# Hybrid mixer: 24 modulation slabs multiplied and halved on GpSimd instead of summed on VectorE

## The reference, cut to what matters

```python
c_act = jax.nn.silu(c)
mod = (c_act @ ada_w[l] + ada_b[l])[:, None, :]
sh_m, sc_m, gt_m, sh_f, sc_f, gt_f = jnp.split(mod, 6, axis=-1)
h = rms_norm(x, norm_mix[l]) * (1 + sc_m) + sh_m
y = hybrid_mixer(h, ...)
x = x + gt_m * y
h = rms_norm(x, norm_ffn[l]) * (1 + sc_f) + sh_f
```

## Time and profile before

| What | Value |
|---|---|
| Median of 3 runs | 3048.45 us (3048.13 to 3048.93) |
| The profiled execution, its own time | 3045.3 us |
| Its span, first to last instruction | 3043.5 us |
| Mean granted TensorE clock | 0.979 |
| Start of the program | 0 to about 50 us |
| Hybrid mixer | about 50 to 508 us |

### The profile page before, as it was taken

The page is one execution under the profiler, slowest core; times in us unless marked ns, Lnnn a source line. Parts: engine busy times, 40 slices in busy tenths (PEclk is TensorE's granted clock), DMA queues, the critical chain, the costliest instruction groups (busy, mean ns, idle before and its releaser), DMA issues.

```text
span 3043.5 us, 32382 instructions
## 1 busy us (share of the span) xinstructions
PE 2888.6 (95%) x13454; PEld 2310.1 (76%) x13454; DVE 1419.6 (47%) x2227; ACT 955.4 (31%) x1276; POOL 442.6 (15%) x345
## 2 busy tenths in 40 slices
PE   6989969999998999999999999899999999999998
PEld 4767657788887878877888877678888865688886
DVE  4474575567534333333232444645444454544353
ACT  3344323321223231233222333432223334332222
POOL 1011011210112211221101100012112100012022
PEclk9999979999999999999999999999999999999999
DMA  5210212446422222222532322112232321122321
GB/s 217 83 56 29 76 56 90 178 161 230 171 81 103 87 73 92 78 83 85 164 110 87 114 77 68 53 69 93 94 111 71 110 68 45 61 98 80 120 80 66
DMA packets 49810, 294.30 MB, mean 97 GB/s; under 512 B 6346, under 2 KB 6474, under 8 KB 23809
## 3 DMA queue, kind: packets, MB, share of 16 engines
q1 hardware_dynamic: 43632, 274.48, 25.2%
q0 software_dynamic: 4736, 15.43, 1.9%
q10 hardware_dynamic: 1296, 2.32, 0.2%
HBM read 283.56 MB, written 8.65 MB: 96 GB/s over the span
## 4 chain that ended last, share of the span: by engine, by line
PE 86%; DVE 7%; ACT 4%; DMA 1%; issue 1%; POOL 0%; SPq 0%; DVEq 0%; ACTq 0%
PE ps L218 86%; DVE ada L399 1%; ACT F L1117 1%; DVE wlo L211 1%; DMA Rf<-in_ada0h 1%; PE ps L1141 1%; DVE F L356 0%; DVE hl L360 0%; DMA F<-in_ada 0%; ACT hh L369 0%; ACT whi L200 0%; DVE F L1108 0%; ACT F L1158 0%; DVE F L2048 0%; DVE F L1153 0%
## 5 line engine op out<-in xcount | busy, mean ns | idle before, releaser
L218 PE MATMUL ps<-hh,whi 128*128 128x512 f32 x2088 | 830.4, 398 | 32.1 <-DVE hl L360 14.5
L218 PE MATMUL ps<-hl,whi 128*128 128x512 f32 x2088 | 819.0, 392 | 0.0
L218 PE MATMUL ps<-hh,wlo 128*128 128x512 f32 x2088 | 818.4, 392 | 0.0
L211 DVE TENSOR_TENSOR wlo<-raw,whi 128x2048 fp32r<-128x2048 f32 (+2 forms) x235 | 492.4, 2096 | 572.4 <-ACT whi L200 567.3
L218 PE MATMUL ps<-R,whi 128*128 128x512 f32 x2080 | 650.6, 392 | 7.8 <-DVE wlo L211 2.8
L200 ACT ACTIVATE whi<-raw 128x2048 fp32r<-128x2048 f32 (+2 forms) x235 | 410.0, 1745 | 727.1 <-PE ps L218 727.0
L218 PEld LDWEIGHTS ps<-hh,whi 128*128 128x128 f32 x2088 | 395.6, 189 | 129.8 <-issue 26.0
L218 PEld LDWEIGHTS ps<-R,whi 128*128 128x128 f32 x2080 | 391.2, 188 | 95.1 <-issue 6.7
L218 PEld LDWEIGHTS ps<-hl,whi 128*128 128x128 f32 x2088 | 395.4, 189 | 84.0
L218 PEld LDWEIGHTS ps<-hh,wlo 128*128 128x128 f32 x2088 | 396.0, 190 | 82.1 <-issue 2.2
L218 PE MATMUL ps<-R,wlo 128*128 128x512 f32 x1040 | 405.2, 390 | 0.0
(11 more groups left out here) (315 smaller groups left out, 2512.2 us busy)
## 6 DMA issues: line engine op xcount, KB each, us to landing
F<-in_ada SPq DMA_DIRECT2D x32, 1024.0 KB, 4.8
raw<-in_fs0in SPq DMA_DIRECT2D x22, 1024.0 KB, 5.4
raw<-in_fs1in SPq DMA_DIRECT2D x22, 1024.0 KB, 4.7
raw<-in_fc0in SPq DMA_DIRECT2D x22, 1024.0 KB, 4.7
raw<-in_fc1in SPq DMA_DIRECT2D x22, 1024.0 KB, 4.7
Rf<-in_ada0h SPq DMA_DIRECT2D x24, 512.0 KB, 3.5
raw<-in_fs0out SPq DMA_DIRECT2D x16, 704.0 KB, 4.6
raw<-in_fs1out SPq DMA_DIRECT2D x16, 704.0 KB, 4.0
```

The costliest lines, as they stand in the source:

```text
L211: e.tensor_tensor(m.wlo[n % 2][:, 0:size], m.raw[m.slot[n]][:, 0:size], m.whi[n % 2][:, 0:size].bitcast(F32), SUB).then_inc(*s.up("wlo", n))
L218: return e.matmul(out, l, r, start=start, stop=stop, skip_group_check=True)
```

## The change

The 24 slabs move from DVE to POOL. For one slab POOL makes one multiply of 128x(8x128), with `csil` broadcast along the 128 columns, written in place, then three adds that halve the block: 4x128, 2x128 and 1x128 columns, the last into `ada`. Each waits for the one before. PE's sum and the bias come once per two slabs. The next load is issued when the last add of a slab has ended. In the plan an ada pair is `pool:4.9 dma:3.4`, `pool:4.9`, `pe:0.3 dve:0.2 dma:3.1`; "dma" is an engine with its own clock, and the chain may begin at 13 us of the plan instead of 1. In the start, `norm 2` is put ahead of the first slab's `whi` and `wlo` on ACT and DVE, and "scale 3" and "turn 3" on PE are put between k = 3 and k = 4 of the mixer's first tiles.

```diff
-    for what in ("scale 0", "scale 1", "norm 0", "scale 2", "norm 1", "slab 0", "norm 2", "scale 3", "norm 3"):
+    for what in ("scale 0", "scale 1", "norm 0", "scale 2", "norm 1", "norm 2", "slab 0", "scale 3", "norm 3"):
...
+def pe_start_end(e, s, m, ready):
+
+    def first_ready(k):
+        if k == 4:
+            pe_start_scale(e, s, m, 3)
+            pe_start_turn(e, s, m, 3)
+        ready(k)
+    return first_ready
...
 def ada_steps():
-    for j in range(16, 41):
-        yield step("pe:0.2 dve:0.2", ("six", "mod", "h", j - 1) if j > 16 else None)
-        if j < 40:
-            yield step("dve:1.8")
-            yield step("dve:1.8")
+    for j in range(16, 40, 2):
+        yield step("pool:4.9 dma:3.4")
+        yield step("pool:4.9")
+        yield step("pe:0.3 dve:0.2 dma:3.1", ("six", "mod", "h", j + 1))
...
-    at, ready, free = [0] * 5, [0.0, 1.0, 1.0, 1.0, 1.0], {"pe": 0.0, "act": 0.0, "dve": 0.0, "pool": 0.0}
+    at, ready, free = [0] * 5, [0.0, 1.0, 1.0, 13.0, 1.0], {"pe": 0.0, "act": 0.0, "dve": 0.0, "pool": 0.0, "dma": 0.0}
...
 def pe_ada_chain(e, s, m):
...
+    for j in range(16, 40, 2):
+        yield from steps(2)
+        six_free(s, "mod", "h", j + 1)
+        s.wait_ge("ada_h", "h", j, 7)
+        pe_ada(e, s, m, j // 2 % 2, 2, 6, ("h", j + 1), "ada_h")
+        yield
...
+def pool_ada_chain(e, s, m):
+    w = m.Rf[:, 4 * T:6 * T].rearrange("p (k n) -> p k n", k=8)
+    for j in range(16, 40):
+        a = m.ada[j // 2 % 2][:, P * (j % 2):P * (j % 2) + P]
+        s.wait_ge("ada_in", j)
+        e.tensor_tensor(w, w, m.csil[:, :].unsqueeze(2).to_broadcast([P, 8, P]), MUL).then_inc(*s.up("ada_h", "h", j, 0))
+        for i, n in ((1, 4), (2, 2)):
+            s.wait_ge("ada_h", "h", j, i - 1)
+            e.tensor_tensor(w[:, 0:n, :], w[:, 0:n, :], w[:, n:2 * n, :], ADD).then_inc(*s.up("ada_h", "h", j, i))
+        s.wait_ge("ada_h", "h", j, 2)
+        s.wait_ge("ada_sum", *(("h", (j - 4) // 2 * 2 + 1) if j >= 20 else ("first", 3)))
+        e.tensor_tensor(a, w[:, 0, :], w[:, 1, :], ADD).then_inc(*s.up("ada_h", "h", j, 7))
+        yield
+        if j % 2:
+            yield
```

More of the change, by code:

```diff
@@ L404, in dve_ada, with pe_ada @@
             yield
-def pe_ada(e, s, m, acc, n, bank, key):
-    s.wait_ge("ada_k", *key, 7)
+def pe_ada(e, s, m, acc, n, bank, key, done="ada_k"):
+    s.wait_ge(done, *key, 7)
     for c in range(n):
@@ L464, in act_start @@
     act_start_norm(e, s, m, 1)
+    act_start_norm(e, s, m, 2)
     act_slab(e, s, m, 0)
-    act_start_norm(e, s, m, 2)
     act_row(e, s, m, 3)
@@ L541, in pe_start @@
     for what in ("shift 0", "squares 0", "shift 1", "scale 0", "turn 0", "shift 2", "scale 1", "turn 1", "scale 2", "turn 2",
-                 "shift 3", "scale 3", "turn 3"):
+                 "shift 3"):
         what, i = what.split()
@@ L555, in pe_start, with pe_start_scale, pe_start_turn @@
         elif what == "scale":
-            if i >= 2:
-                s.wait_ge("mod", "first", i - 2)
-            pe_ada(e, s, m, i % 2, 2, 3 + i % 2, ("first", i))
-        else:
[L560 to L565, removed]
+            pe_start_scale(e, s, m, i)
+        else:
+            pe_start_turn(e, s, m, i)
+def pe_start_scale(e, s, m, i):
+    if i >= 2:
+        s.wait_ge("mod", "first", i - 2)
+    pe_ada(e, s, m, i % 2, 2, 3 + i % 2, ("first", i))
+def pe_start_turn(e, s, m, i):
+    if i >= 2:
+        s.wait_ge("mod", "shift", i - 2)
+    s.wait_ge("mod_row", i)
+    for c in range(2):
+        t = mm(e, m.ps[5 + i % 2][:, c:c + 1], first_row(m, i)[:, c * P:(c + 1) * P], m.k("ones")[0:1, 0:1])
+    t.then_inc(*s.up("mod_turn", i))
+def pe_start_end(e, s, m, ready):
[5 more added lines that the diff above has]
+    return first_ready
 FFN = {"s0": ("fs0", 0, False), "s1": ("fs1", 1, False), "c0": ("fc0", 0, True), "c1": ("fc1", 1, True)}
@@ L1993, in pe_gdn_pre @@
         pe_dense_free(s, m, n)
-        yield from pe_tiles(e, s, m, n, (0, 1), m.h, ready)
+        if n == 0:
+            yield from pe_tiles(e, s, m, n, (0, 1), m.h, pe_start_end(e, s, m, ready))
+        else:
+            yield from pe_tiles(e, s, m, n, (0, 1), m.h, ready)
         yield from steps(2)
@@ L2302, in act_gdn_head @@
     if h == 2:
-        s.wait_ge("ada_k", "h", 39, 7)
+        s.wait_ge("ada_h", "h", 39, 7)
     e.activation(m.o(h)[0], qT, ACT.Copy).then_inc(*s.up("o_hi", "hyb", h))
@@ L2671, in dve_ada_chain @@
 def dve_ada_chain(e, s, m):
-    for j in range(16, 41):
-        if j > 16:
-            dve_ada_bias(e, s, m, j - 1, 1, 6, "ada_sum", ("h", j - 1))
+    for j in range(16, 40, 2):
+        yield from steps(2)
+        dve_ada_bias(e, s, m, j, 2, 6, "ada_sum", ("h", j + 1))
         yield
[L2676 to L2680, removed]
+def pool_ada_chain(e, s, m):
[12 more added lines that the diff above has]
+        if j % 2:
@@ L2681, in dve_ada_chain @@
             yield
 def sp_ada_chain(e, s, m):
+    s.wait_ge("mod_mm", 3)
+    s.wait_ge("ada_k", "first", 3, 7)
+    sp_ada(e, s, m, 16)
     for j in range(16, 40):
[L2686 to L2693, removed]
+        yield
+        if j < 39:
+            s.wait_ge("ada_h", "h", j, 7)
+            sp_ada(e, s, m, j + 1)
+        if j % 2:
+            yield
@@ L2699, in pe_hybrid, with sp_ada @@
+def sp_ada(e, s, m, j):
+    e.dma_start(m.Rf[:, 4 * T:6 * T], m.dram["ada0h"][j - 16]).then_inc(*s.dma("ada_in", j))
 def pe_hybrid(e, s, m):
@@ L2703, in act_hybrid @@
 def act_hybrid(e, s, m):
-    merged(act_gdn(e, s, m, 0), act_gdn(e, s, m, 1), act_stick(e, s, m), steps(73), act_gdn_gates(e, s, m))
+    merged(act_gdn(e, s, m, 0), act_gdn(e, s, m, 1), act_stick(e, s, m), steps(36), act_gdn_gates(e, s, m))
 def dve_hybrid(e, s, m):
@@ L2711, in pool_hybrid @@
 def pool_hybrid(e, s, m):
-    merged(pool_gdn(e, s, m, 0), pool_gdn(e, s, m, 1), pool_stick(e, s, m), steps(73), steps(len(GATE_STEPS)))
+    merged(pool_gdn(e, s, m, 0), pool_gdn(e, s, m, 1), pool_stick(e, s, m), pool_ada_chain(e, s, m), steps(len(GATE_STEPS)))
 def sp_hybrid(e, s, m):
```

## The result

The changed kernel takes 3030.33 us in the median of four runs (3026.43 to 3033.55), the kernel before 3048.29 us: a ratio of 0.9941, with a 95% interval of 0.9924 to 0.9958, or 18 us faster. The forecast was 20 us, 3028 us. The profiled execution is the slowest of the four, 3033.55 us for a span of 3031.7 us, so the trace shows 11.8 of the 18 us.

A forecast was written before the change was run, and what follows sets the result against it. The prediction took PE, busy 95% of the span, as the bound, idling most from 376 to 508 us; -4.3 (start) + 3 (early stretch) - 18.9 (last stretch) = -20.2 us gave 3028 us, range 3006 to 3046 us.

The forecast's parts named there:

- The sum: Whole program: start -4.3, early stretch +3 and last stretch -18.9 give -20.2 us, so 3028 us against the median.
- The start: Before the mixer's first tiles: PE does k = 0 to 3 in its 8.59 us gap, gaining 4.3 us.
- the cover: In the start: k = 6 and 7 wait for `norm 3`, which is late next if the gap no longer hides it.
- POOL's cost: A slab's multiply and three adds on POOL: 5.1 us, or a period of about 8.9 us with its load.
- The early stretch: Mixer, 100 to 350 us: POOL work stalls DVE while slabs leave it; between -5 and +4 us, taken as +3.
- the lock's rival: Early stretch: every POOL microsecond stops DVE, +15 instead of +3, so -8 in all, 3040 us; chance 0.17.
- The last stretch: Mixer, 376 to 508 us: L2067 10.9 us, slabs inside DVE bursts 5 us, clock 3 us; together -18.9 us.
- No slab after 350 us: Sign of being right: no POOL slab after about 350 us, all fourteen slabs out of the last stretch.
- PE standing for POOL's sums: Rival: load and POOL outlast the 9.05 us a slab PE's queue expects; at 11 us, 3075 us; chance 0.12.
- The reserve of 9.05 us a slab: Plan's 8.3 us a slab with queues 9% behind, against the forecast 8.9; PE's wait for sums costed at nothing.
- The plan's order: All queues: new costs reorder them, which no row can price; 10 us allowed to either side.

The follow-up runs named there:

- start_only: The kernel before with the changed start alone (norm 2 ahead of the first slab's split, scale 3 and turn 3 between k = 3 and k = 4): 3044.21 us, ratio 0.9999.
- after_again: The changed kernel itself measured once more, on another chip: 3030.76 us, ratio 0.9944.
- pool_short: The changed kernel without each slab's multiply and first two adds, so the modulation's second half is not computed: 3012.99 us, ratio 0.9894.
- pool_long: The changed kernel with each slab's multiply done twice on POOL, plan unchanged: 3039.14 us, ratio 0.9972.
- dve_pairs: The changed kernel with each slab's eight instructions back on DVE, 3.1 us in the plan; pairs, load clock and start kept: 3034.91 us, ratio 0.9964.
- slabs_early: The changed kernel with the slab chain given the highest priority in the plan: 3020.22 us, ratio 0.9911.
- no_clock_early: The changed kernel with no load in the plan and the slab chain first (no_load_clock and slabs_early together): 3091.32 us, ratio 1.0147.
- no_load_clock: The changed kernel with no load in the plan and the chain's start at 1 instead of 13 us: 3020.28 us, ratio 0.9912.

## Why the prediction was right, point by point

- **The sum** was -20.2 us; measured -18, by the marks -13.3 in a trace that is 3 us slower than the median. That it held is in part luck: two terms were wrong by 7 and 14 us in opposite ways.
- **The start**, -4.3: the mark gives -3.7 (372.89 to 369.20), but on its own it is worth nothing in the time. "If the cover is gone, `norm 3` is late next" was right too: PE waits 0.3 us at k = 7. That the later waits take it back was not in the forecast.
- **POOL's cost**, 5.1 us a slab: 5.4, with a multiply of 1.89 us at best, 2.14 in the mean, where the line through two sizes gave 2.34. POOL was to be busy 115 to 130 us more: 126.6. A slab with its load takes 8.8 us where little disturbs it (multiplies at 138.34 and 147.12 us), forecast 8.9.
- **The early stretch**, +3, with +4 as its upper end: this is the term that failed. Against start_only it is 385.94 - 369.20 = +16.7 us (+14.5 by after_again), of which pool_short shows 11.5 to 13.8 to be the multiply and two adds. That is the size which the lock's rival gave this term, +15; the rival's total failed only because the last stretch gave more. DVE is busy 172.48 us up to the mark and 153.88 in pool_short, 18.6 us apart. That is inside the 0 to 52, but well under the 46 that the chosen +3 stands for. What was wrong is the price of 0.18 us of PE per us of DVE: it is 13.8 / 18.6 = 0.74, or 11.5 / 18.2 = 0.63 by after_again. The 0.18 was PE's whole idle time over DVE's whole busy time, an average that counts every DVE instruction with slack; the stall seen above hits a `wlo` and a convolution, on whose results later matmuls of PE wait. A fixed price would be wrong too: in pool_long 16.9 us more of DVE cost 4.6 us in this stretch, 0.27 for one. pool_short's two stretches:

```profile
41.00:372.18 331.18, 299.87 (x1499) 235.98 (x1497) 153.88 (x245) 133.23 (x195) 47.69 (x61) 0.94 0.24 83
372.18:478.48 106.30, 95.98 (x594) 79.74 (x593) 51.91 (x103) 44.53 (x80) 22.70 (x24) 0.94 0.05 17
```

  PE idles 35.8 us in the changed kernel and 31.3 here, 4.5 us apart, and its busy time differs by 9.3 us, at a granted clock of 0.92 and 0.94. By after_again it is 7.6 us of idle time and 3.9 us of busy time, at 0.93. Both kinds of loss are there; their shares are not settled.
- **The last stretch**, -18.9: -26.3. L2067's 10.9 us went as forecast, but they go in dve_pairs too. PE's idle time fell by 18.3 us, from 30.1 to 11.7, more than the 16 that I took, and PE's busy time by 8.0 us where I allowed 3 for the clock (0.85 to 0.92).
- **No slab after 350 us**: wrong. Five stand after 376 us; slabs_early, which changes the chain's priority in the plan alone, has the last one at 287 us. The working had a slip as well: its upper end, 343 us from about 50 us on, ends at 393 and not before 376. slabs_early shows that the five cost nothing in the last stretch. The forecast's reason, "which takes all fourteen out", holds for nine of them. dve_pairs, with eight of them gone and all on DVE, shows this to be the larger part, 15.9 of the 26.3 us; the rest came off DVE by the change of engine, which gives the other 10.4.
- **PE standing for POOL's sums**, cost nothing: right, no such wait is in the changed kernel's rows from 50 to 505 us. The reserve of 9.05 us a slab was not a sound figure, though: one `wlo` planned 9% short does not stretch the whole plan by 9%. The rival is real all the same, as no_clock_early shows.
- **The plan's order**, 10 us to either side: no_load_clock and slabs_early are both 10 us faster with the same instructions.

What stays open: why those two orders win 6 to 8.6 us in the early stretch. It shows as a higher granted clock and not as less idle time of PE, and no run isolates a place. Either of them is faster than both kernels, at 0.991 of the kernel before.

## What to carry to other kernels

Work that stands in DVE's queue ahead of short serial steps is dear there, and there are two ways out: plan it earlier, or give it to another engine. Here the last stretch became 26 us shorter, 16 with eight slabs fewer in it and 10 more with the rest on POOL. Another engine is not free: POOL's work on 24 slabs cost 12 to 14 us in the dense stretch, where it holds off DVE instructions with two SBUF inputs. Price a stall at what stands behind the stalled instruction, not at an average of idle over busy time, and count the clock with it. Test the order apart from the work: it was worth 10 us with the same instructions, and a plan that puts the slabs first without knowing their loads cost 71 us.

## What the runs showed of the hardware

- A POOL multiply of 128x1024 with one operand broadcast along the inner 128 columns takes 1.89 us at best. Adds of two full operands take 0.45, 0.72 and 1.26 us for 128, 256 and 512 columns, and a line through them gives 2.34 us for 1024. No run shows whether it is the broadcast, the operation or the size that makes the difference.
- DVE and POOL held each other off by whole instructions where both inputs of DVE's lay in SBUF: a `wlo` of 2.29 us became 3.62 us, and two adds of together 1.98 us became 4.35 us. Over the early stretch 93 us more of POOL stretched DVE by 18.6 us.
- Eight ACT instructions of 128x128 with a column as scale, 391 ns each in the mean, took 2.44 us in a row, so they overlap; one POOL instruction did the same in 1.9 us.
- The same matmuls of the same kernel were busy 309.17 us in one execution and 303.75 in another, at a granted clock of 0.92 and 0.93.
